# Mixture-of-experts stage: indirect gathers with a bound, results scattered to one row per token and choice

## The reference, cut to what matters

```python
g_idx = jnp.argmax(g_logits, axis=-1)
top_v, top_i = lax.top_k(e_logits, TOP_K_IN_GROUP)              # 2 of 8 experts
wts = g_prob[:, None] * jax.nn.softmax(top_v, axis=-1)
eid = (g_idx[:, None] * EXPERTS_PER_GROUP + top_i).reshape(-1)  # 1024 pairs
...
def expert_block(args):
    tok_b, e = args
    xb = xpad[tok_b]                                            # rows of 1024 f32
    h = jax.nn.silu(xb @ w_gate[e]) * (xb @ w_up[e])            # 1024 -> 512
    return h @ w_down[e]                                        # 512 -> 1024
y = jnp.zeros((t + 1, d)).at[buf_tok].add(out * buf_wt)         # to the tokens
```

## Time and profile before

| | |
|---|---|
| median of 3 runs | 1641.99 us (1640.69 to 1642.13) |
| profiled execution, its own time | 1646.2 us |
| its span in the trace | 1644.4 us |
| TensorE busy | 1402.5 us, 85% of the span |
| VectorE, ScalarE, GpSimd busy | 658.6, 484.5, 93.6 us |
| HBM read, written | 321.56 MB, 24.64 MB |

### The profile page before, as it was taken

How to read it: one execution, slowest core, us unless ns; L and a number is a source line. 1 busy time by engine, 2 the same in 40 slices (tenths; PEclk the granted TensorE clock), 3 DMA queues, 4 the chain that set the end, 5 groups by cost and what they waited for, 6 DMA issues and landing times.

```text
span 1644.4 us, 17162 instructions
## 1 busy us (share of the span) xinstructions
PE 1402.5 (85%) x6530; PEld 944.2 (57%) x6530; DVE 658.6 (40%) x1136; ACT 484.5 (29%) x718; POOL 93.6 (6%) x155
## 2 busy tenths in 40 slices
PE   6999985697876778977728999988999999999976
PEld 5786774232222223322216888766788788878765
DVE  4552887000000000000044756455546554655545
ACT  5452512010000000100044231324445444443432
POOL 2000010110000000100020110000000000000000
PEclk9998996899898889998969999999999999999988
DMA  9720279899999999999964553221221212121001
GB/s 354 299 103 1 92 253 382 307 375 401 393 403 386 398 383 401 382 381 396 410 253 186 205 211 133 74 108 51 68 87 64 91 52 102 52 103 52 1 1 64
DMA packets 39852, 347.71 MB, mean 211 GB/s; under 512 B 5952, under 2 KB 6080, under 8 KB 21440
## 3 DMA queue, kind: packets, MB, share of 16 engines
q1 hardware_dynamic: 26176, 292.11, 45.5%
q0 software_dynamic: 12608, 51.42, 9.2%
q10 hardware_dynamic: 960, 2.70, 0.4%
HBM read 321.56 MB, written 24.64 MB: 211 GB/s over the span
## 4 chain that ended last, share of the span: by engine, by line
PE 44%; DVE 3%; ACT 2%; issue 1%; DMA 1%; DVEq 0%; POOL 0%; SPq 0%; ACTq 0%; POOLq 0%
PE ps L256 43%; PE ps L645 1%; ACT ar L794 0%; DVE b_NL L1238 0%; DMA ar<-y_scratch,rt 0%; DVE ar L1230 0%; PE ps L704 0%; DVE hres L1643 0%; ACT ar L807 0%; PE ps L262 0%; DVE hres L1636 0%; DMA y_scratch<-ar 0%; ACT b_NH L803 0%; DVE ar L1823 0%; ACT ar L1008 0%
## 5 line engine op out<-in xcount | busy, mean ns | idle before, releaser
L256 PE MATMUL ps<-ar 128*128 128x128 f32 (+6 forms) x1038 | 251.0, 442 | 30.5 <-ACT ar L938 8.5
L256 PE MATMUL ps<-ring,ar 128*64 128x512 f32 x720 | 220.6, 637 | 55.3 <-issue 48.7
L256 PE MATMUL ps<-b_NH,b_WH 128*128 128x512 f32 x768 | 201.7, 399 | 12.0 <-ACT b_NH L803 6.2
L1585 DVE TENSOR_TENSOR ar<-ar,ps 128x256 f32<-128x256 f32 x34 | 14.3, 421 | 483.1 <-ACT ar L935 483.1
L256 PE MATMUL ps<-b_NH,b_WL 128*128 128x512 f32 x768 | 195.2, 390 | 0.0
L256 PE MATMUL ps<-b_NL,b_WH 128*128 128x512 f32 x768 | 189.7, 389 | 0.0
L256 PEld LDWEIGHTS ps<-ring,ar 128*64 128x64 f32 x720 | 68.8, 147 | 194.0 <-issue 185.9
L1171 DVE TENSOR_TENSOR b_WL<-ring,b_WH 128x1024 fp32r<-128x1024 f32 x112 | 136.7, 1221 | 98.1 <-ACT b_WH L746 98.0
L256 PEld LDWEIGHTS ps<-ar 128*128 128x128 f32 (+3 forms) x1038 | 125.6, 175 | 83.2 <-issue 53.8
L256 PEld LDWEIGHTS ps<-b_NH,b_WH 128*128 128x128 f32 x768 | 141.1, 189 | 42.8 <-ACT b_NH L803 11.1
L256 PEld LDWEIGHTS ps<-b_NH,b_WL 128*128 128x128 f32 x768 | 144.7, 188 | 30.2
(11 more groups left out here) (252 smaller groups left out, 1563.1 us busy)
## 6 DMA issues: line engine op xcount, KB each, us to landing
ring<-in_wts_dram SPq DMA_DIRECT2D x80, 2048.0 KB, 15.5
spare<-in_wts_dram SPq DMA_DIRECT2D x30, 2048.0 KB, 36.8
ar<-in_wts_dram SPq DMA_DIRECT2D x22, 2048.0 KB, 37.7
ar<-in_wmod_dram POOLq DMA_DIRECT2D x16, 768.0 KB, 6.0
ar<-in_wmod_dram POOLq DMA_DIRECT2D x24, 512.0 KB, 4.1
y_scratch<-gate POOLq DMA_DIRECT2D x11, 1024.0 KB, 21.2
y_scratch<-ar SPq DMA_DIRECT2D x68, 128.0 KB, 31.2
hres<-in_x_dram SPq DMA_DIRECT2D x4, 512.0 KB, 5.8
```

The source lines that it names most:

```text
L256: return pe.matmul(o, l, m, start=start, stop=stop, skip_group_check=True)
L1585: return dve.tensor_tensor(hh[s], sg[s], ps[:, b, 256:512], ALU.mult)
```

## The change

1. The zero fill of `y_scratch` and the wait for it go.
2. `y_scratch` gets 2,048 rows of 2 KB: row ((choice x 512 + token) x 2 + half). The masks carry 2 x (choice x 512 + token) + 2 instead of the token's number, for 128 partitions instead of 64 (lower half of a row in partitions 0 to 63, upper half in 64 to 127), and VectorE makes two tables of it: `row_i` (rows of `y_scratch` for the scatter) and `tab_i` (tokens for the gather).
3. The gathers get `bounds_check=511` (a row whose index is above it is left out). The gather of the second block is issued for every expert, without a branch.
4. The results are stored by one indirect DMA of GpSimd per block (`scatter`, 128 partitions, `bounds_check=2047`) instead of two plain ones of SyncE. In the branch without a second block GpSimd issues a small DMA for the semaphore `oy`.
5. The eight last loads of results are plain DMAs.

```diff
-        y_d = nc.dram_tensor("y_scratch", [NSLOT, D], F32, kind="Internal").ap()
+        y_d = nc.dram_tensor("y_scratch", [2048, 512], F32, kind="Internal").ap()
...
-                t = mm(ps[0:CAP, 6, 0:NBLK], Jm[:, c, :], Bm[:, c, :], c == 0, c == 7)
+                t = mm(ps[:, 6, 0:NBLK], Jm[:, c, :], Bm[:, c, :], c == 0, c == 7)
...
-            signals(dve.tensor_tensor(Jm, bc(last(lo_f), 128, 8, CAP), bc(mid(i_n[:, 0:CAP]), 128, 8, CAP),
+            dve.wait_ge(S["xz"], 4)
+            signals(dve.tensor_tensor(Jm, bc(last(lo_f), 128, 8, 128), bc(mid(slot), 128, 8, 128),
                                       ALU.is_equal), "jb")
             for c in range(8):
-                signals(dve.tensor_scalar(Bm[:, c, :], i_n, gs8[:, c:c + 1], tokid[:, c % 4:c % 4 + 1], ALU.is_equal,
+                signals(dve.tensor_scalar(Bm[:, c, :], i_n, gs8[:, c:c + 1], tokid[:, c:c + 1], ALU.is_equal,
                                           ALU.mult), "jb")
...
-            signals(dve.tensor_copy(tab_i[0:CAP, :], ps[0:CAP, 6, 0:NBLK]), "tab")
+            signals(dve.tensor_scalar(empty, ps[:, 6, 0:NBLK], 0.0, 8192.0, ALU.is_equal, ALU.mult))
+            behind()
+            signals(dve.scalar_tensor_tensor(out=row_i, in0=ps[:, 6, 0:NBLK], scalar=half, in1=empty, op0=ALU.add,
+                                             op1=ALU.add))
+            behind()
+            signals(dve.tensor_scalar(tab_i, row_i, 1, 4607, ALU.arith_shift_right, ALU.bitwise_and))
+            behind()
+            signals(dve.tensor_scalar(tab_i[0:CAP, 0:2], tab_i[0:CAP, 0:2], 511, None, ALU.bitwise_and), "tab")
...
-            pool.memset(gz, 0.0).then_inc(S["const"], 1)
-            pool.wait_ge(S["const"], 4)
-            pool.wait_ge(s_slot[3], 16)
-            yz = y_d[NE * CAP:NSLOT, :].rearrange("(p r) d -> p (r d)", p=128)
-            for c in range(11):
-                pool.dma_start(yz[:, c * 2048:(c + 1) * 2048], gz).then_inc(S["yzero"], 16)
...
+            pool.iota(ii[:, 0:8], pattern=[[1024, 2], [256, 4]], base=2, channel_multiplier=2).then_inc(S["pc"], 1)
...
+            pool.memset(half, -1.0).then_inc(S["xz"], 1)
+            pool.wait_ge(S["xz"], 3)
+            pool.memset(half[0:64, :], -2.0).then_inc(S["xz"], 1)
...
                 return pool.indirect_dma_start(
                     out=xg[s][0:64, :], out_offset=None, in_=xn_d,
-                    in_offset=bass.IndirectOffsetOnAxis(ap=tab_i[0:64, n:n + 1], axis=0))
+                    in_offset=bass.IndirectOffsetOnAxis(ap=tab_i[0:64, n:n + 1], axis=0),
+                    bounds_check=511, oob_is_err=False)
+
+            def scatter(s, n):
+                return pool.indirect_dma_start(
+                    out=y_d, out_offset=bass.IndirectOffsetOnAxis(ap=row_i[:, n:n + 1], axis=0),
+                    in_=ysb[s], in_offset=None, bounds_check=2047, oob_is_err=False)
...
                 if n < NE:
-                    with pool.If(second(n)):
-                        if n:
-                            pool.wait_ge(S["o_g"], 16 * n)
-                            pool.wait_ge(S["o_tx"], n)
-                        gather(2, NE + n).then_inc(S["o_g"], 16)
+                    if n:
+                        pool.wait_ge(S["o_g"], 16 * n)
+                        pool.wait_ge(S["o_tx"], n)
+                    gather(2, NE + n).then_inc(S["o_g"], 16)
+                if n:
+                    m = n - 1
+                    pool.wait_ge(S["m_y"], m + 1)
+                    scatter(m % 2, m).then_inc(S[f"y{m % 2}"], 16)
+                    pool.wait_ge(S["o_y"], m + 1)
+                    with pool.If(second(m)):
...
+                        scatter(2, NE + m).then_inc(S["oy"], 16)
                     with pool.Else():
-                        if n:
-                            pool.wait_ge(S["o_g"], 16 * n)
-                            pool.wait_ge(S["o_tx"], n)
-                        pool.dma_start(xg[2][0:16, 0:16], xn_d[0:16, 0:16]).then_inc(S["o_g"], 16)
+                        if m:
+                            pool.wait_ge(S["oy"], 16 * m)
+                        pool.dma_start(rt[0:16, 8:16], xn_d[0:16, 0:8]).then_inc(S["oy"], 16)
...
-                sp.wait_ge(S["m_y"], n + 1)
-                for t in store(n, n % 2):
-                    t.then_inc(S[f"y{n % 2}"], 16)
```

More of the change, by code:

```diff
@@ L82, in program @@
         cs = sb("cs", [128, 8])
[L83 removed]
+        rt = sb("rt", [128, 184])
         top = ExitStack()
@@ L188, in program @@
         iot, i_n, blk_f, lo_f, sl_f = small(32 + NBLK), small(NBLK), small(8), small(8), small(8)
-        Jm, Bm = small(8, 64), small(8, NBLK)
+        Jm, Bm, slot = small(8, 128), small(8, NBLK), small(128)
         sc1, EM, POS, CNT = small(4, 32), small(4, 32), small(4, 32), small(32)
@@ L204, in program @@
         ctl = rt[:, 92:108].bitcast(I32)
-        tokid = rt[:, 108:112]
+        row_i = rt[:, 108:108 + NBLK].bitcast(I32)
+        tokid, half, empty = small(8), small(1), small(NBLK)
         ov = [area(0, 4096), area(4096, 4096)]
@@ L1883, in gpsimd_program @@
             pool.tensor_copy(thr[:, 0:8], e64[:, 1:9]).then_inc(S["pc"], 1)
-            pool.iota(ii[:, 0:4], pattern=[[128, 4]], base=0, channel_multiplier=1).then_inc(S["pc"], 1)
+            pool.iota(ii[:, 0:8], pattern=[[1024, 2], [256, 4]], base=2, channel_multiplier=2).then_inc(S["pc"], 1)
             pool.wait_ge(S["pc"], 8)
-            pool.tensor_copy(tokid, ii[:, 0:4]).then_inc(S["pc"], 1)
+            pool.tensor_copy(tokid, ii[:, 0:8]).then_inc(S["pc"], 1)
+            pool.tensor_copy(slot[:, 0:64], i_n[:, 0:64]).then_inc(S["xz"], 1)
+            pool.tensor_copy(slot[:, 64:128], i_n[:, 0:64]).then_inc(S["xz"], 1)
+            pool.memset(half, -1.0).then_inc(S["xz"], 1)
+            pool.wait_ge(S["xz"], 3)
+            pool.memset(half[0:64, :], -2.0).then_inc(S["xz"], 1)
+            pool.wait_ge(S["xz"], 4)
             pool.memset(oneb, 1.0).then_inc(S["pc"], 1)
@@ L1904, in gpsimd_program @@
                 gather(n, n).then_inc(S[f"g{n}"], 16)
+            pool.memset(xg[2][0:64, :], 0.0).then_inc(S["xz"], 1)
+            pool.wait_ge(S["xz"], 5)
             for n in range(NE + 1):
@@ L1926, in gpsimd_program @@
                         pool.wait_ge(S["o_tx"], NE + j)
+                    pool.wait_ge(S["o_g"], 16 * (NE + j))
                     gather(2, 2 * NE + j).then_inc(S["o_g"], 16)
-                    pool.wait_ge(S["oy"], 32 * (NE + j + 1))
+                    pool.wait_ge(S["o_y"], NE + j + 1)
+                    pool.wait_ge(S["oy"], 16 * (NE + j))
+                    scatter(2, 2 * NE + j).then_inc(S["oy"], 16)
+                    pool.wait_ge(S["oy"], 16 * (NE + j + 1))
             pool.wait_ge(S["m_d2"], NE)
             pool.wait_ge(S["m_y"], NE)
[L1933 to L1936, removed]
+            pool.wait_ge(S["y0"], 16 * (NE // 2))
+            pool.wait_ge(S["y1"], 16 * (NE // 2))
+            pool.wait_ge(S["oy"], 16 * NE)
+            y_v = y_d.rearrange("(c p i h) d -> c p i (h d)", c=2, p=4, i=128)
             for m in range(8):
[L1938 to L1942, removed]
+                pool.dma_start(yg[m], y_v[m % 2, m // 2]).then_inc(s_yg[m], 16)
             pool.dma_start(gate[:, 1, :], row(R_BG + 1024, 1024)).then_inc(S["bias"], 16)
@@ L1984, in sync_program @@
             load(P_MOE + 8)
[L1986 to L1990, removed]
             for n in range(NE):
@@ L2028, in sync_program @@
                     expert(0, 2).then_inc(S["v_w0"], 16)
-                    sp.wait_ge(S["o_y"], NE + j + 1)
-                    for t in store(2 * NE + j, 2):
-                        t.then_inc(S["oy"], 16)
             sp.wait_ge(S["m_d2"], NE)
```

19 lines of the change are left out of this document (10 added, 9 removed).

## The result

The changed kernel takes 1696.1 us (median of 4 runs, 1691.71 to 1698.85), the kernel before 1641.34 us beside it (4 runs, 1639.92 to 1642.13). The ratio is 1.0332, with a 95% interval of 1.0312 to 1.0352: slower by 54.8 us, where +41.8 was forecast.

What follows compares the result with a forecast made beforehand. The prediction took DMA to bound the experts' stage. New gathers +49.3, stores -8, start +1.5 and end -1 us summed to +41.8, from 1641.99 to 1683.8 us, with a range of 1664 to 1704 us.

Steps and rivals of the forecast that it cites:

- What bounds the kernel: Experts' stage, 311 to 826 us: DMA share 1.01, so each DMA microsecond added or removed moves the end by one.
- Part 1: Index table: an empty slot becomes 4095 & 4607 = 511, within the gather's bound, so no gather leaves out a row.
- Part 2: Second block's gathers in the experts' stage: 30 new full ones, 29 in the saturated stretch at 1.7 us, +49.3 us.
- Part 3: Result stores in the experts' stage: 20.1 us of stores replaced by scatters of 11.8 us at the zero fill's rate, -8 us.
- Part 4: Start: wider first mask and four operations for one conversion bring the table, first gather and first slot release 1.5 us later.
- Part 5: End: scatter and small DMA +0.5, plain loads in place of indirect ones about -1.5, together -1 us.
- Part 6: Zero fill, SyncE's waits and GpSimd's new order: claimed to cost nothing, the gather staying hidden with at least 6 us left.
- What the profile after would show: Profile: 64 gathers, reads about 329.4 MB, writes about 8.4, DMA share 1.0, stage end about 40 us later, `copy_y` awaiting `down`.
- A: Rival on the gathers: empty rows are left out after all, -37.0 us, 1605 us; chance 0.07.
- B: Rival on the new gathers: they cost only their bytes, 17.7 us instead of 49.3, +10.2, 1652 us; chance 0.06.
- C: Rival on the stage: gathers at 2.1 us each and scatters at a gather's price, +68.5, 1710 us; chance 0.08.
- D: Rival on the stage: the DMA stretch is not what is late, no change within 0.2%; chance 0.02.

Runs made afterwards that it cites:

- e1: Changed kernel with the mark of an empty slot 8194 instead of 8192, so gathers leave empty rows out: 1613.31 us, ratio 0.9811 to the kernel before.
- e2: Changed kernel with the branch around the second block's gather put back, so the 30 new gathers go: 1639.78 us, ratio 0.9974 to the kernel before.
- e3: Kernel before, its gathers leaving out empty rows from the third block on; stores, zero fill and branch kept: 1614.01 us, ratio 0.9811.
- e7: Changed kernel; without a second block, the second gather fetches 128 pieces of 2 KB into 128 partitions: 1657.75 us, ratio 1.0081 to the kernel before.
- e10: e2 with all 34 gathers into 128 partitions, four transposes instead of eight, no row left out: 1596.88 us, ratio 0.9719 to the kernel before.
- e11: Changed kernel; without a second block, the second gather is two of 2 KB pieces into partitions 0 to 63: 1698.3 us, ratio 1.0339 to the kernel before.
- e9: e1 with each first scatter followed by a second one into another scratch: 1631.08 us, ratio 0.9911 to the kernel before.
- e12: Kernel before, with each first block stored a second time into another scratch: 1662.12 us, ratio 1.0116.
- e5: e1 with the branch around the second block's gather put back as in e2: 1612.62 us, ratio 0.9817 to the kernel before.

## Why the prediction was right in direction and short by a quarter

**What bounds the kernel** held. In every kernel the DMA share of the stage is 0.98 to 1.01, and the time follows what the gathers cost there.

**Part 1, the table**, held, and decided the case. e1 shows it: two added to the mark, and 85 us are gone.

**Part 2, the new gathers**: the mechanism was right, the price short. 29 x 1.7 = 49.3 us was forecast; taking only these gathers out (e2) shows 58.6 us, 1.95 each, inside the bound of 2.1. By the stage's 29 it is 2.02. The 1.7 came from windows of 4 us, in which a gather need not lie whole; that this is the reason is argued, not shown. Of the old gathers, e3 got back 29.5 us for 29.5 forecast, but its interval (27.8 to 34.4 us) also holds the 33.8 that 1.95 a gather would give. By the Trainium skill (DMA: Bandwidth & Descriptors, The descriptor swizzle) half of the engines write partitions 0 to 63 in a transfer to all 128; the half rate, and with the earlier trace rows the 1.2 us, is what I made of it. I weighed that against the windows and went by the windows. On the price that was right: 1.2 us is too little by 0.7. But the section points at the cause: with all 128 partitions written (e7, e10) the gathers cost about their bytes, and 2 KB pieces into 64 partitions (e11) do not. What these runs show beyond it is that writing partitions 0 to 63 alone costs more than twice the bytes' time beside a saturated stream of weights: 1.95 / 0.61 = 3.2 times. Why it is more than twice is not shown.

**Part 3, the stores**: mis-sized. The stores were priced well: 66 of 131 KB at 2.25 us a MB are 19.5 us (20.1 forecast). The scatters look mis-sized: 4.19 MB at 4.0 us a MB are 16.9 us in the place of 11.8. The term is then -2.6, not -8. The interval of e9 alone still holds the 2.8 us a MB of the forecast; that e2 has the rest of the change at -3.8 us, with -7.5 just outside its interval, points the same way. The step that failed is the choice of the zero fill as the nearest row, "since a scatter reads from 128 partitions as it does": a block with few tokens has its rows in few partitions of each half, and pieces of 2 KB. Which of the two makes it dear was not tried.

**Part 4, the start**: +1.5 forecast, and the trace has the first release 3.35 us earlier. VectorE's operations don't show in it; the first gather reached TensorE 4.1 us after its issue in the place of 7.8. In all profiled kernels whose gathers have a bound and whose first `turn_x` was read it was 3.6 to 4.9 us, in the kernel before and e12 7.8 and 7.2. What they share and those two lack is the bound and the clearing of `xg[2]` behind the first two gathers (e3 has both, with fill and stores as before); how either would shorten the wait is open. The size in one trace says little anyhow: the first gather's issue lies between 289.2 and 294.9 us in kernels that are the same up to there.

**Part 5, the end**: -1 forecast; from the last `copy_y` to the first `pick` 12.1 us after 11.6. The scatter's 1.03 us and the eight plain loads in 4.22 us are as thought, but no gain shows: the first load is issued 7.9 us after the last `copy_y`, where it was 6.0.

**Part 6** held: neither the zero fill nor SyncE's waits nor the new order on GpSimd cost or gave anything that shows; e3, which keeps fill and stores, stands beside e1. The zero fill alone was not tried.

The sum on the medians: 58.6 of gathers, -2.6 of stores and scatters, and -1.2 of start, end and what can't be told apart give the 54.8 measured. The forecast had 49.3, -8 and +0.5. The 13.0 us missing are 9.3 of the gathers' price, 5.4 of the scatters', and -1.7 of the rest.

**What the profile after would show.** The 64 gathers, the reads of 329.4 MB and `copy_y` waiting for `down` came as said. The writes did not: 13.11 MB where 8.4 were forecast, since that counter takes in the rows left out.

The rivals: A (rows left out after all, 1605 us) was priced within some 8 us, e1 taking 1613; by e3 its gather term was about right, so the difference is put down to the scatters again, which is argued. B falls with e2 and e7: the gathers cost their bytes only when they are wide. C (1710 us) had the better price for the gathers: its 60.9 us can't be told from the 58.6 measured. Its scatters were too dear, 27.2 us against 16.9. The time lies between the forecast's and its own. D falls with the first row of the windows. The time was inside the range.

## What to carry to other kernels

In a stage that DMA bounds, price an indirect load by the partitions it writes and not by its bytes alone: into partitions 0 to 63 this one cost 1.95 us, into all 128 about 0.6 to 0.7, and making all 34 wide was worth 43 us with no row left out (e10 over e2). A mark that is to survive index arithmetic must be followed through it in integers with the worst offset; one bit lost here turned -30 us into +55, with the 30 new gathers behind it. And a counter of bytes may count what the program asked for: read the queue's MB when the question is whether rows were moved.

## What the runs showed that I had not expected

- Gathers of which every row is left out are as good as free here: 30 of them changed the median by 0.7 us (e1 against e5), by the intervals at most some 0.2 us each.
- The page's HBM read and written MB include rows that were left out (329.41 MB in the changed kernel and in e1, 13.11 MB written where 4.7 MB less were moved); the MB of the queue don't, though its packets are as many.
- A scatter of 2 KB rows costs 4.0 us a MB beside the weights (2.5 to 5.5), a plain store 2.25 (1.8 to 2.7).
- With wide gathers the stage moves 415 GB/s (e10) where the kernel before has 391, at nearly the same DMA share.
